# The mixer's output projection as three products of rounded high and low parts, with the normed rows kept whole and divided at the head of the up-projection

## The chip, the cores and the metric

The kernel runs on one core of one Trainium2 chip. The metric is the device time of one launch in microseconds (us). The time before is 4591.77 us, the median of three runs (4585.16 to 4597.04).

## The reference

One inference step of one layer of a hybrid decoder, all in float32: a prompt of 2048 tokens and 8 decode tokens, model width 1024. What matters here is the seam between the token mixer and the feed-forward part:

```python
mixed = jnp.concatenate([o_gdn, o_dsa.astype(o_gdn.dtype)], axis=-1)
x = x + jnp.einsum('bte,ed->btd', mixed, w_out[l])
h = rms_norm(x, norm_ffn[l])
u, ffn_buf = causal_dwconv(jnp.einsum('btd,df->btf', h, w_up[l]), ffn_buf, ffn_conv_w[l])
gate, up = jnp.split(u + ffn_conv_b[l], 2, axis=-1)
x = x + jnp.einsum('btf,fd->btd', jax.nn.silu(gate) * up, w_down[l])
```

`w_out` is 1024 x 1024, `w_up` 1024 x 5632, `w_down` 2816 x 1024.

## The kernel before, in words

The kernel is a row of phases, each a block with its own semaphores and buffers. Between two phases all engines meet in a barrier; SP clears the old phase's semaphores and then, in `credit`, raises each of the new phase's by 4 before its first load. All waits of a phase are for 4 and more.

The phase `mix` (lines 679 to 815) does the output projection, the residual sum, the norm and the transposition. It works on 17 tiles of 128 tokens, sixteen of the prompt and one that holds the 8 decode tokens, with two buffers b = 0, 1 in turn. ScalarE's queue loads `w` (4 MB) whole. For a tile SP loads `m` (the mixed rows, transposed, 512 KB) and `x` (512 KB). TensorE's `multiply` (L730) does for 8 slices k of the contraction and 2 halves of 512 columns one float32 matmul, `m`'s slice stationary and `w` moving. A float32 matmul stands in the trace as two records. VectorE adds the residual (L794), SP stores the sum (L715) and loads the buffer's next `m` and `x`. ScalarE squares and sums (L761), VectorE and ScalarE work out the root and its inverse, VectorE scales the row (L802), TensorE's `turn` (L744) transposes it in 8 pieces, VectorE multiplies by the gain into `h` (L807). ScalarE rounds `h` to the type fp32r into `ht_high` (L767), and POOL writes the rest, `h` less that, to `ht_low` (L781). TensorE's order is multiply(j, 1), turn(j, 0), multiply(j+1, 0), turn(j, 1), in a loop over j; each engine's order is written out by hand in the same way.

The phase `ffn_up` (from L818) makes 22 pairs of 128 gate and up channels. Its weights are loaded 512 KB at a time, rounded by ScalarE (L949 for the first, L926 later) and POOL subtracts (L960). All 2056 token columns are taken in five groups of 412 (the first one 408) in the order 4, 0, 1, 2, 3, each into a PSUM bank of its own, with 8 slices x 3 products of rounded parts (high x high, high x low, low x high, L914). ScalarE empties the banks (L932), and VectorE does the causal convolution. After the third group TensorE transposes some history (`side`, L892), which waits for the first bank to be emptied. `ffn_down` multiplies in the same manner, in the form 128 x 128 weights, 512 moving columns (L1151 to L1153); its weights' low parts come from VectorE (L1161), and those of its activations from POOL (L1123).

## Time and profile before

| | |
|---|---|
| median of three runs | 4591.77 us |
| the profiled execution | 4549.66 us |
| its span, first to last instruction | 4548.4 us |
| mean granted TensorE clock | 0.902 |
| TensorE matmul busy | 3964.1 us, 87% |
| TensorE weight loads busy | 3133.7 us, 69% |
| VectorE busy | 2130.7 us, 47% |
| ScalarE busy | 1527.5 us, 34% |
| GpSimd (POOL) busy | 689.2 us, 15% |

The profile is of one execution. PE is TensorE's matmuls, PEld its weight loads, DVE VectorE, ACT ScalarE, POOL GpSimd, SP the engine that issues most transfers; SPq and ACTq are DMA issues on the queues of SP and ScalarE. "L736" is line 736 of the kernel. After a row's numbers stands in brackets how long the engine was idle ahead of it, and what released it. The granted clock is a share of full speed: 1.00 is 2.4 GHz, 0.50 is 1.2 GHz. The mixer's phase lies between 2713 and 2989 us of the span, the up-projection up to 4000 us, the down-projection behind it.

### The profile page before, as it was taken

What the parts mean: (1) busy time and instruction counts of PE and PEld (TensorE: products, weight loads), DVE (VectorE), ACT (ScalarE), POOL (GpSimd) and SP (SyncE); (2) the same over time, 40 slices, a digit from 0 to 9 for tenths busy, and PEclk for the clock granted to TensorE, in tenths of its full rate; (3) what the DMA queues carried; (4) which work ended last, traced back from release to release, by engine and by line L of the source; (5) the groups of instructions that cost most, each with busy time, mean ns of one, the idle gap of its engine ahead of it and who ended that gap; (6) DMA issues with size and microseconds to landing.
All of it is one profiled execution on the core that took longest, in us unless ns stands there. A gap on an engine that the chain in (4) does not pass through costs nothing. (4 is left out here: it accounts for less than half of the span.)

```text
span 4548.4 us, 51075 instructions
## 1 busy us (share of the span) xinstructions
PE 3964.1 (87%) x19290; PEld 3133.7 (69%) x19290; DVE 2130.7 (47%) x4240; ACT 1527.5 (34%) x2433; POOL 689.2 (15%) x547
## 2 busy tenths in 40 slices
PE   7789787798769876888888769989999999979999
PEld 4445454455358555777777764479999999958777
DVE  5528988998943683333333332224444444430200
ACT  2115555665645233333333321122222222221211
POOL 0100000000000003222222121111111111124443
PEclk9889898999879687778788789999999999989999
DMA  2242222121142102111111013311212121145433
GB/s 92 78 108 64 59 56 69 35 70 36 45 165 73 36 11 69 30 29 33 29 33 31 25 58 107 102 44 37 56 37 56 37 56 37 47 152 168 130 111 112
DMA packets 286836, 298.41 MB, mean 66 GB/s; under 512 B 33599, under 2 KB 231103, under 8 KB 281626
## 3 DMA queue, kind: packets, MB, share of 16 engines
q1 hardware_dynamic: 271278, 256.80, 19.7%
q0 software_dynamic: 2112, 20.97, 1.2%
q10 hardware_dynamic: 13264, 18.25, 1.2%
q8 instruction: 110, 1.80, 0.2%
q14 instruction: 72, 0.59, 0.0%
HBM read 202.15 MB, written 94.10 MB: 65 GB/s over the span
## 5 line engine op out<-in xcount | busy, mean ns | idle before, releaser
L530 PE MATMUL chan_p_g<-ht,chan_w 128*128 128x412 f32 (+1 forms) x1760 | 678.0, 528 | 62.7 <-ACT chan_flat L578 33.7
L914 PE MATMUL up_p_g<-ht_high,up_wh 128*128 128x412 f32 (+1 forms) x1760 | 617.0, 351 | 0.0
L914 PE MATMUL up_p_g<-ht_low,up_wh 128*128 128x412 f32 (+1 forms) x1760 | 615.0, 349 | 0.0
L914 PE MATMUL up_p_g<-ht_high,up_wl 128*128 128x412 f32 (+1 forms) x1760 | 614.8, 349 | 0.0
L530 PEld LDWEIGHTS chan_p_g<-ht,chan_w 128*128 128x128 f32 x1760 | 341.5, 197 | 310.1 <-issue 230.1
L932 ACT ACTIVATE up_pre<-up_p_g 128x412 f32<-128x412 f32 (+1 forms) x220 | 113.3, 515 | 748.0 <-PE up_p_g L914 748.0
L1294 ACT ACTIVATE chan_signed<-chan_sc,chan_trial 128x512 bf16<-128x512 f32 (+6 forms) x224 | 304.9, 1361 | 148.5 <-DVE chan_trial L1349 127.7
L914 PEld LDWEIGHTS up_p_g<-ht_high,up_wh 128*128 128x128 f32 x1760 | 331.3, 188 | 1.6 <-issue 0.4
L914 PEld LDWEIGHTS up_p_g<-ht_low,up_wh 128*128 128x128 f32 x1760 | 331.2, 188 | 1.2
L914 PEld LDWEIGHTS up_p_g<-ht_high,up_wl 128*128 128x128 f32 x1760 | 331.0, 188 | 0.5
L984 DVE TENSOR_SCALAR up_acc<-up_pre,up_taps 128x2048 f32<-128x2048 f32 x44 | 59.3, 1347 | 573.5 <-ACT up_pre L932 573.5
L1335 DVE TENSOR_SCALAR_CACHE_REDUCE chan_tie<-chan_sc,chan_trial 128x384 bf16<-128x384 f32 (+6 forms) x224 | 316.2, 1412 | 7.6
L1270 PE MATMUL chan_p_sc<-ik,chan_iq 128*128 128x512 f32 (+3 forms) x304 | 187.7, 621 | 101.0 <-ACT chan_r L1289 90.9
L1151 PE MATMUL down_p_y<-down_wh,down_ah 128*128 128x512 f32 x704 | 274.4, 390 | 0.0
L1152 PE MATMUL down_p_y<-down_wl,down_ah 128*128 128x512 f32 x704 | 274.2, 390 | 0.0
L1153 PE MATMUL down_p_y<-down_wh,down_al 128*128 128x512 f32 x704 | 274.1, 389 | 0.0
L1123 POOL TENSOR_TENSOR down_al<-down_a,down_ah 128x1024 fp32r<-128x1024 f32 x88 | 211.7, 2405 | 359.8 <-ACT down_ah L1097 359.8
L736 PE MATMUL mix_p_y<-mix_w,mix_m 128*128 128x512 f32 x544 | 237.9, 596 | 22.7 <-DMA mix_m<-scratch_mix 22.7
L960 POOL TENSOR_TENSOR up_wl<-up_w,up_wh 128x1024 fp32r<-128x1024 f32 x44 | 128.7, 2927 | 838.8 <-ACT up_wh L926 830.1
L1289 ACT ACTIVATE chan_r<-chan_p_sc 128x512 f32<-128x512 f32 (+3 forms) x304 | 159.6, 543 | 222.9 <-PE chan_p_sc L1271 115.4
L1097 ACT ACTIVATE down_ah<-down_a 128x1024 fp32r<-128x1024 f32 x88 | 93.3, 1060 | 386.6 <-PE down_p_y L1153 373.6
L736 PEld LDWEIGHTS mix_p_y<-mix_w,mix_m 128*128 128x128 f32 x544 | 102.8, 191 | 146.6 <-issue 146.6
(549 smaller groups left out, 6874.9 us busy)
## 6 DMA issues: line engine op xcount, KB each, us to landing
down_a<-scratch_act SPq DMA_DIRECT2D x88, 512.0 KB, 3.7
scratch_act<-up_acc SPq DMA_DIRECT2D x22, 1028.0 KB, 5.2
up_w<-in_w_up SPq DMA_DIRECT2D x44, 512.0 KB, 6.4
chan_iq<-scratch_iq SPq DMA_DIRECT2D x28, 512.0 KB, 7.2
scratch_qkv<-chan_acc SPq DMA_DIRECT2D x12, 1028.0 KB, 4.6
mid_raw<-scratch_qkv SPq DMA_DIRECT2D x16, 768.0 KB, 5.3
chan_w<-in_w_in SPq DMA_DIRECT2D x22, 512.0 KB, 4.6
proj_x<-in_x_prompt SPq DMA_DIRECT2D x16, 512.0 KB, 3.5
```

The lines of the kernel that those rows point to most:

```text
L530: last = pe.matmul(p_g[u % BANKS][:, 0:cols.stop - cols.start], weights[:, k, :], K.ht[:, k, cols], start=(k == 0), stop=(k == KD - 1))
L736: last = pe.matmul(p_y[b][:, half, :], m[b][:, k, :], w[:, k, half * 512:(half + 1) * 512], start=(k == 0), stop=(k == KD - 1))
L914: last = pe.matmul(p_g[u][:, 0:cols.stop - cols.start], wp[s][:, k, :], hp[:, k, cols], start=(k == 0 and m == 0), stop=(k == KD - 1 and m ...
L960: pool.tensor_tensor(wl[s][:, :, :], w[s][:, :, :], wh[s][:, :, :].bitcast(F32), ALU.subtract).then_inc(s_wl[s], 1)
L1123: pool.tensor_tensor(al[t % RING][:, :, :], a[t % RING][:, :, :], ah[t % RING][:, :, :].bitcast(F32), ALU.subtract)\
L1151: pe.matmul(bank[0:m, :], hi, wh[:, f, :], start=(f == 0), stop=False)
L1152: pe.matmul(bank[0:m, :], hi, wl[:, f, :], start=False, stop=False)
L1153: last = pe.matmul(bank[0:m, :], lo, wh[:, f, :], start=False, stop=(f == NF - 1))
L1270: pe.matmul(out, self.iq[b][:, 0, h, :], self.K.ik2[:, cols], start=True, stop=False)
L1289: act.activation(self.r[n % self.RING][:, 0:width], self.p_sc[n % 2][:, 0:width], ACT.Relu).then_inc(S["relu"], 1)
L1294: act.activation(self.signed[:, 0:nk], self.sc[1][:, 0:nk], ACT.Sign, scale=-1.0, bias=self.trial[:, 1:2].bitcast(F32), accum_out=self.sig ...
L1335: last = dve.tensor_scalar(self.tie[:, 0:na], self.sc[0][:, 0:na], trial[:, 0:1].bitcast(F32), None, ALU.is_ge, ALU.add, accum_out=count[: ...
```

## The change

In `mix` the weights and each tile of `m` are divided into a part rounded to fp32r (ScalarE: `wh`, `mh`) and the rest (VectorE: `wl`, `ml`, written where `w` and `m` had landed). `multiply` does three matmuls of fp32r for each k and half: high x high, high x low, low x high. `w` is loaded in eight slices, and the first tile's multiply waits for them one after the other. There is one buffer `xn` instead of two, and the square's output goes there. POOL has no work left in the phase; `h` and its two parts are gone, and the scaled transposed rows are written whole to `h_full`. In `ffn_up` ScalarE rounds `h_full` in five parts (one per group of columns) into `K.ht`, and VectorE subtracts in place, `K.hl` lying on `h_full`. The first channel pair of TensorE's loop is written out so that each group waits for its own part. `m`'s first loads, the residual loads and the stores stay as they are on SP.

```diff
@@ -681,17 +681,22 @@
 
     with phase(nc, "mix") as (c, stack):
         two = lambda name, shape, dt=F32: [c.sb(f"{name}{b}", shape, dt) for b in range(2)]
-        w = c.sb("w", [P, KD, D])
-        m, x, xn = two("m", [P, KD, P]), two("x", [P, D]), two("xn", [P, D])
-        junk, h = c.sb("junk", [P, D], BF16), c.sb("h", [P, KD, P])
+        with ExitStack() as landing:
+            lands = Ctx(nc, landing, "mix")
+            w = lands.sb("w", [P, KD, D])
+            m = [lands.sb(f"m{b}", [P, KD, P]) for b in range(2)]
+        wl, ml = c.sb("wl", [P, KD, D], F32R), two("ml", [P, KD, P], F32R)
+        wh, mh, x = c.sb("wh", [P, KD, D], F32R), two("mh", [P, KD, P], F32R), two("x", [P, D])
+        xn = c.sb("xn", [P, D])
         stat = two("stat", [P, 4])
         gain = c.sb("gain", [P, KD])
         p_y = [c.ps(f"y{b}", [P, 2, 512]) for b in range(2)]
         p_t = [c.ps(f"t{b}", [P, KD, P]) for b in range(2)]
-        s_w = c.sem("w")
-        s_m, s_x, s_mm, s_x2, s_sum, s_mean, s_root, s_inv, s_norm, s_turn, s_ht, s_st = (
-            c.sems(n) for n in "m x mm x2 sum mean root inv norm turn ht st".split())
-        s_high, s_low = c.sem("high"), c.sem("low")
+        s_w = c.sems("w", KD)
+        s_gain, s_wh, s_wl = c.sem("gain"), c.sem("wh"), c.sem("wl")
+        s_m, s_mh, s_ml, s_x, s_mm, s_x2, s_sum, s_mean, s_root, s_inv, s_norm, s_ht, s_st = (
+            c.sems(n) for n in "m mh ml x mm two sum mean root inv norm ht st".split())
+        s_turn = c.sem("turn")
         block = open_block(nc, stack, c)
         LAST = NT // 2
 
@@ -699,7 +704,7 @@
         def _(sp):
             credit(sp, c)
             sp.dma_start(gain[:, :], norm_ffn.rearrange("(k p) -> p k", p=P), allow_slow_non_contiguous=True)\
-              .then_inc(s_w, 16)
+              .then_inc(s_gain, 16)
 
             def load(j, b, n=P):
                 rows = ds(j * 256 + b * P, P) if n == P else slice(SEQ, TOK)
@@ -728,23 +733,25 @@
 
         @block.tensor
         def _(pe):
-            def multiply(j, b):
-                pe.wait_ge(s_m[b], 4 + j * 16 + 16)
+            def multiply(j, b, first=False):
+                pe.wait_ge(s_ml[b], 4 + j + 1)
                 pe.wait_ge(s_x2[b], 4 + j)
                 for k in range(KD):
-                    for half in range(2):
-                        last = pe.matmul(p_y[b][:, half, :], m[b][:, k, :], w[:, k, half * 512:(half + 1) * 512],
-                                         start=(k == 0), stop=(k == KD - 1))
+                    if first:
+                        pe.wait_ge(s_wl, 4 + k + 1)
+                    for i, (mp, wp) in enumerate(((mh, wh), (mh, wl), (ml, wh))):
+                        for half in range(2):
+                            last = pe.matmul(p_y[b][:, half, :], mp[b][:, k, :], wp[:, k, half * 512:(half + 1) * 512],
+                                             start=(k == 0 and i == 0), stop=(k == KD - 1 and i == 2))
                 last.then_inc(s_mm[b], 1)
 
             def turn(j, b):
                 pe.wait_ge(s_norm[b], 4 + j + 1)
                 pe.wait_ge(s_ht[b], 4 + j)
                 for k in range(KD):
-                    last = pe.transpose(p_t[b][:, k, :], xn[b][:, k * P:(k + 1) * P], K.ident[:, :])
-                last.then_inc(s_turn[b], 1)
-            pe.wait_ge(s_w, 4 + 32)
-            multiply(0, 0)
+                    last = pe.transpose(p_t[b][:, k, :], xn[:, k * P:(k + 1) * P], K.ident[:, :])
+                last.then_inc(s_turn, 1)
+            multiply(0, 0, True)
             with pe.Fori(0, LAST) as j:
                 multiply(j, 1)
                 turn(j, 0)
@@ -754,39 +761,40 @@
 
         @block.scalar
         def _(act):
-            act.dma_start(w[:, :, :], w_out.rearrange("(k p) n -> p k n", p=P)).then_inc(s_w, 16)
+            for k in range(KD):
+                act.dma_start(w[:, k, :], w_out[k * P:(k + 1) * P, :]).then_inc(s_w[k], 16)
+
+            def split(j, b, n=P):
+                act.wait_ge(s_m[b], 4 + j * 16 + 16)
+                act.activation(mh[b][:, :, 0:n], m[b][:, :, 0:n], ACT.Copy).then_inc(s_mh[b], 1)
 
             def stats(j, b):
                 act.wait_ge(s_x2[b], 4 + j + 1)
-                act.activation(junk[:, :], x[b][:, :], ACT.Square, accum_out=stat[b][:, 0:1]).then_inc(s_sum[b], 1)
+                act.wait_ge(s_turn, 4 + j * 2 + b)
+                act.activation(xn[:, :], x[b][:, :], ACT.Square, accum_out=stat[b][:, 0:1]).then_inc(s_sum[b], 1)
                 act.wait_ge(s_mean[b], 4 + j + 1)
                 act.activation(stat[b][:, 2:3], stat[b][:, 1:2], ACT.Sqrt).then_inc(s_root[b], 1)
 
-            def high(j, b, n=P):
-                act.wait_ge(s_ht[b], 4 + j + 1)
-                act.activation(K.ht[:, :, ds(j * 256 + b * P, n)], h[:, :, 0:n], ACT.Copy).then_inc(s_high, 1)
+            split(0, 0)
+            for k in range(KD):
+                act.wait_ge(s_w[k], 4 + 16)
+                act.activation(wh[:, k, :], w[:, k, :], ACT.Copy).then_inc(s_wh, 1)
+            split(0, 1)
             stats(0, 0)
-            with act.Fori(0, LAST) as j:
+            with act.Fori(0, LAST - 1) as j:
+                split(j + 1, 0)
                 stats(j, 1)
-                high(j, 0)
+                split(j + 1, 1)
                 stats(j + 1, 0)
-                high(j, 1)
-            high(LAST, 0, DEC)
-
-        @block.gpsimd
-        def _(pool):
-            def low(j, b, n=P):
-                cols = ds(j * 256 + b * P, n)
-                pool.wait_ge(s_high, 4 + j * 2 + b + 1)
-                pool.tensor_tensor(K.hl[:, :, cols], h[:, :, 0:n], K.ht[:, :, cols].bitcast(F32), ALU.subtract).then_inc(s_low, 1)
-            with pool.Fori(0, LAST) as j:
-                low(j, 0)
-                low(j, 1)
-            low(LAST, 0, DEC)
+            split(LAST, 0, DEC)
+            stats(LAST - 1, 1)
+            stats(LAST, 0)
 
         @block.vector
         def _(dve):
-            dve.wait_ge(s_w, 4 + 32)
+            def lower(j, b, n=P):
+                dve.wait_ge(s_mh[b], 4 + j + 1)
+                dve.tensor_tensor(ml[b][:, :, 0:n], m[b][:, :, 0:n], mh[b][:, :, 0:n].bitcast(F32), ALU.subtract).then_inc(s_ml[b], 1)
 
             def norm(j, b):
                 dve.wait_ge(s_x[b], 4 + j * 16 + 16)
@@ -798,21 +806,32 @@
                 dve.wait_ge(s_root[b], 4 + j + 1)
                 dve.reciprocal(stat[b][:, 3:4], stat[b][:, 2:3]).then_inc(s_inv[b], 1)
                 dve.wait_ge(s_inv[b], 4 + j + 1)
-                dve.wait_ge(s_turn[b], 4 + j)
-                dve.tensor_scalar(xn[b][:, :], x[b][:, :], stat[b][:, 3:4], None, ALU.mult).then_inc(s_norm[b], 1)
-
-            def scale(j, b):
-                dve.wait_ge(s_turn[b], 4 + j + 1)
-                dve.wait_ge(s_low, 4 + j * 2 + b)
-                dve.tensor_tensor(h[:, :, :], p_t[b][:, :, :],
-                                  gain[:, :].unsqueeze(2).broadcast_to([P, KD, P]), ALU.mult).then_inc(s_ht[b], 1)
+                dve.tensor_scalar(xn[:, :], x[b][:, :], stat[b][:, 3:4], None, ALU.mult).then_inc(s_norm[b], 1)
+
+            def scale(j, b, n=P):
+                dve.wait_ge(s_turn, 4 + j * 2 + b + 1)
+                dve.tensor_tensor(K.h_full[:, :, ds(j * 256 + b * P, n)], p_t[b][:, :, 0:n],
+                                  gain[:, :].unsqueeze(2).broadcast_to([P, KD, n]), ALU.mult).then_inc(s_ht[b], 1)
+            lower(0, 0)
+            for k in range(KD):
+                dve.wait_ge(s_wh, 4 + k + 1)
+                dve.tensor_tensor(wl[:, k, :], w[:, k, :], wh[:, k, :].bitcast(F32), ALU.subtract).then_inc(s_wl, 1)
+            lower(0, 1)
+            dve.wait_ge(s_gain, 4 + 16)
             norm(0, 0)
-            with dve.Fori(0, LAST) as j:
+            with dve.Fori(0, LAST - 1) as j:
+                lower(j + 1, 0)
                 norm(j, 1)
                 scale(j, 0)
+                lower(j + 1, 1)
                 norm(j + 1, 0)
                 scale(j, 1)
-            scale(LAST, 0)
+            lower(LAST, 0, DEC)
+            norm(LAST - 1, 1)
+            scale(LAST - 1, 0)
+            norm(LAST, 0)
+            scale(LAST - 1, 1)
+            scale(LAST, 0, DEC)
 
 
 def ffn_up(nc, K, w_up, conv_w, conv_b, conv_state, outs):
@@ -836,7 +855,7 @@
         p_g = [c.ps(f"g{g}", [P, 512]) for g in range(5)]
         p_x = [c.ps(f"x{s}", [P, 2, P]) for s in range(2)]
         p_taps = c.ps("taps", [P, 4, P])
-        S = {n: c.sem(n) for n in ("slab zero tturn taps mm free hist step silu res state").split()}
+        S = {n: c.sem(n) for n in ("parth partl slab zero tturn taps mm free hist step silu res state").split()}
         s_w, s_past, s_st = c.sems("w"), c.sems("past"), c.sem("st")
         s_wh, s_wl, s_conv = c.sems("wh"), c.sems("wl"), c.sems("conv")
         wv = w_up.rearrange("(k p) n -> p k n", p=P)
@@ -900,7 +919,7 @@
                 pe.transpose(p_x[s][0:lead + 2 + DEC, 1, :], pre[s][:, SEQ - lead:SEQ + 2 + DEC], K.ident[:, :])\
                   .then_inc(S["hist"], 1)
 
-            with pe.Fori(0, NF // 2) as j:
+            def channel_pair(j, first=False):
                 for b in range(2):
                     n = j * 2 + b
                     for s in range(2):
@@ -908,6 +927,8 @@
                         parts = ((wh, K.ht), (wh, K.hl), (wl, K.ht))
                         for u, g in enumerate(ORDER):
                             cols = cols_of(g)
+                            if first and b == 0 and s == 0:
+                                pe.wait_ge(S["partl"], 4 + u + 1)
                             pe.wait_ge(S["free"], 8 + n * 10 + s * 5 + u - 4)
                             for k in range(KD):
                                 for m, (wp, hp) in enumerate(parts):
@@ -916,6 +937,9 @@
                             last.then_inc(S["mm"], 1)
                             if u == 2:
                                 side(j, b, s)
+            channel_pair(0, True)
+            with pe.Fori(1, NF // 2) as j:
+                channel_pair(j)
 
         @block.scalar
         def _(act):
@@ -944,9 +968,17 @@
                             act.activation(acc[0][:, :], acc[0][:, :], ACT.Silu).then_inc(S["silu"], 1)
                     if not last:
                         split(n + 1, s)
+            def part(u):
+
+                cols = cols_of(ORDER[u])
+                act.activation(K.ht[:, :, cols], K.h_full[:, :, cols], ACT.Copy).then_inc(S["parth"], 1)
+            part(0)
             for s in range(2):
                 act.wait_ge(s_w[s], 4 + 16)
                 act.activation(wh[s][:, :, :], w[s][:, :, :], ACT.Copy).then_inc(s_wh[s], 1)
+                part(1 + s)
+            part(3)
+            part(4)
             act.wait_ge(S["zero"], 4 + 4)
             with act.Fori(0, NF - 1) as n:
                 copies(n, False)
@@ -961,11 +993,19 @@
 
         @block.vector
         def _(dve):
+            def lower(u):
+
+                cols = cols_of(ORDER[u])
+                dve.wait_ge(S["parth"], 4 + u + 1)
+                dve.tensor_tensor(K.hl[:, :, cols], K.h_full[:, :, cols], K.ht[:, :, cols].bitcast(F32), ALU.subtract)\
+                   .then_inc(S["partl"], 1)
             for s in range(2):
                 dve.memset(pre[s][:, 0:2], 0.0)
             dve.memset(slab[:, :, :], 0.0).then_inc(S["zero"], 2)
             for b in range(2):
                 dve.memset(past[b][:, :, :], 0.0).then_inc(S["zero"], 1)
+            for u in range(5):
+                lower(u)
             dve.wait_ge(S["tturn"], 4 + 1)
             dve.tensor_copy(taps[:, :, :, :].rearrange("p i s m -> p i (s m)"), p_taps[:, :, 0:2 * NF]).then_inc(S["taps"], 1)
             dve.wait_ge(S["taps"], 4 + 1)
@@ -3165,9 +3205,12 @@
                 K.empty = keep("empty", [P, QUARTERS, PAIRS], F32, rule)
                 heads(nc, K, ins, outs)
         with ExitStack() as hidden:
-            K.ht, K.hl = keep("ht_high", [P, KD, TOK], F32R, hidden), keep("ht_low", [P, KD, TOK], F32R, hidden)
+            with ExitStack() as whole:
+                K.h_full = keep("ht_full", [P, KD, TOK], F32, whole)
+            K.hl = keep("ht_low", [P, KD, TOK], F32R, hidden)
             mix(nc, K, ins["x_prompt"].rearrange("b t d -> (b t) d"), ins["x_sample"].rearrange("b t d -> (b t) d"),
                 ins["w_out"].rearrange("l k n -> (l k) n"), ins["norm_ffn"].rearrange("l d -> (l d)"))
+            K.ht = keep("ht_high", [P, KD, TOK], F32R, hidden)
             ffn_up(nc, K, ins["w_up"].rearrange("l k n -> (l k) n"), ins["ffn_conv_w"].rearrange("l j n -> (l j) n"),
                    ins["ffn_conv_b"].rearrange("l n -> (l n)"), ins["state_ffn_conv"].rearrange("l b j n -> (l b j) n"), outs)
         ffn_down(nc, K, ins["w_down"].rearrange("l f n -> (l f) n"), outs)
```

## Rows read from the trace of the kernel before

**Rows 1.** Page, costliest groups: records, busy us, mean ns of one, idle before.
```profile
L1151 PE MATMUL down_p_y<-down_wh,down_ah 128*128 128x512 f32 x704 | 274.4, 390 | 0.0
...
L736 PE MATMUL mix_p_y<-mix_w,mix_m 128*128 128x512 f32 x544 | 237.9, 596 | 22.7 <-DMA mix_m<-scratch_mix 22.7
```

**Rows 2.** Table by stretches: us, each engine's busy us, granted clock, DMA share, GB/s.
```profile
2744.75:2977.46 232.71, 232.71 (x633) 109.49 (x632) 53.73 (x79) 37.48 (x63) 35.24 (x15) 1.00 0.33 100
2977.50:2989.00 11.50, 2.85 (x17) 2.21 (x15) 4.65 (x6) 2.66 (x5) 2.66 (x2) 0.68 0.02 3
3022.00:3044.60 22.60, 22.60 (x124) 22.50 (x123) 8.42 (x7) 6.73 (x8) 2.97 (x1) 1.00 0.00 1
4031.00:4548.00 517.00, 509.83 (x2242) 408.27 (x2241) 68.48 (x55) 110.58 (x107) 209.33 (x87) 1.00 0.44 138
```

**Rows 3.** Timeline, one mixer tile: start us, us, engine, line, operation, count.
```profile
2949.12 13.90 PE L736 MATMUL mix_p_y<-mix_w,mix_m 128*128 128x512 f32 x32
...
2962.86 1.04 PE L744 MATMUL mix_p_t<-ident,mix_xn 128*128 128x128 f32 x8
...
2963.73 13.90 PE L736 MATMUL mix_p_y<-mix_w,mix_m 128*128 128x512 f32 x32
```

**Rows 4.** Timeline, down-projection: products of rounded parts, 48 from first to last.
```profile
4250.01 0.39 PE L1151 MATMUL down_p_y<-down_wh,down_ah 128*128 128x512 f32 x1
4250.02 0.19 PEld L1152 LDWEIGHTS down_p_y<-down_wl,down_ah 128*128 128x128 f32 x1
...
4260.89 0.39 PE L1151 MATMUL down_p_y<-down_wh,down_ah 128*128 128x512 f32 x1
```

**Rows 5.** Timeline, mixer: multiply's end (first transpose), next load of the same buffer.
```profile
2948.25 1.04 PE L744 MATMUL mix_p_t<-ident,mix_xn 128*128 128x128 f32 x8
...
2950.10 0.43 SPq L707 DMA_DIRECT2D mix_m<-scratch_mix  x1
```

**Rows 6.** Answer on the tile mix_m: from issue of a load to landing.
```profile
DMA to landing us min/median/max: 2.9/4.6/8.9
```

**Rows 7.** Groups by shape: whole-tile operations of VectorE and ScalarE.
```profile
L995 DVE TENSOR_TENSOR up_acc<-up_acc 128x2056 f32<-128x2056 f32 x22 | 50.6, 2299 | 0.8
...
L926 ACT ACTIVATE up_wh<-up_w 128x1024 fp32r<-128x1024 f32 x42 | 44.3, 1054 | 0.0
...
L944 ACT ACTIVATE up_acc<-up_acc 128x2056 f32<-128x2056 f32 x22 | 42.4, 1926 | 0.2
```

**Rows 8.** Answer on line 1161: subtraction of 1024 elements, ns min/median/max.
```profile
L1161 DVE TENSOR_TENSOR down_wl<-down_w_next,down_wh x11: 1211/2583/2584, 4234.0 to 4292.0; 128x1024 fp32r<-128x1024 f32 x11
```

**Rows 9.** Timeline, first product of the mixer.
```profile
2729.06 29.43 PE L736 MATMUL mix_p_y<-mix_w,mix_m 128*128 128x512 f32 x64 [22.73 <-DMA mix_m<-scratch_mix]
```

**Rows 10.** Timeline, end of the mixer and head of the up-projection.
```profile
2981.53 1.85 PE L744 MATMUL mix_p_t<-ident,mix_xn 128*128 128x128 f32 x8 [3.03 <-DVE mix_xn L802]
...
2988.01 0.32 POOL L781 TENSOR_TENSOR ht_low<-mix_h,ht_high 128x64 fp32r<-128x64 f32 x1 [1.69 <-ACT ht_high L767]
2989.01 0.09 DVE L965 MEMSET up_pre<- 128x2 f32 x2 [1.37 <-PEq L136]
...
2991.80 1.02 SPq L863 DMA_DIRECT2D up_w<-in_w_up  x2
...
2999.50 0.29 PEld L914 LDWEIGHTS up_p_g<-ht_high,up_wh 128*128 128x128 f32 x1 [0.40 <-issue]
```

**Rows 11.** Timeline, down-projection's first whole products, before the clock rose.
```profile
4031.20 0.63 PE L1151 MATMUL down_p_y<-down_wh,down_ah 128*128 128x512 f32 x1
...
4032.91 0.44 PE L1152 MATMUL down_p_y<-down_wl,down_ah 128*128 128x512 f32 x1
```

**Rows 12.** Timeline of ScalarE, up-projection: table load, first two banks emptied.
```profile
2998.84 1.28 ACT L932 ACT_TABLE_LOAD   x1
3005.50 0.51 ACT L932 ACTIVATE up_pre<-up_p_g 128x408 f32<-128x408 f32 x1 [5.37 <-PE up_p_g L914]
3009.99 0.52 ACT L932 ACTIVATE up_pre<-up_p_g 128x412 f32<-128x412 f32 x1 [3.97 <-PE up_p_g L914]
```

## The prediction

> **What bounds the kernel now.** I began with the page's table of engines and its costliest groups. TensorE is busy for 87% of the span, and the output projection is one of its larger groups: 544 matmul records at L736 with 237.9 us busy, against 704 records each for the down-projection's three products [rows 1]. The mean of one record (596 ns here, 390 ns there) is no price: records overlap, so only the distance from one start to the next is.
>
> Next came the table by stretches [rows 2]. From 2744.75 to 2977.46, the last sixteen of the seventeen tiles, TensorE is busy for 232.71 of 232.71 us at granted clock 1.00, while VectorE has 53.7 us and ScalarE 37.5. The stage is bound by TensorE alone. The up-projection behind it is the same, 22.60 of 22.60 us. Between the two TensorE is nearly idle: 2.85 us busy of the 11.5 from 2977.5 to 2989, and its first product of the up-projection comes only at 2999.50. So four places can move the end: the projection's matmuls, its first tile, its last, and the head of the up-projection.
>
> **Part 1, the steady matmuls.** In the timeline one tile of before runs from 2949.12 to 2963.73, 14.61 us [rows 3]: 32 records in 13.73 us (each single precision matmul leaves two, so 0.429 us apart, 0.858 per product), then eight transposes in 0.87. The new tile issues 16 x 3 = 48 products of rounded parts. The nearest row is the down-projection, same types, 128 weight columns, 512 moving columns: 48 of them go from 4250.01 to 4260.89, 0.2267 us apart [rows 4]. So a tile multiplies in 48 x 0.2267 = 10.88 us instead of 13.73. The bounds of the new pitch: at best that of the old passes halved, 0.429 / 2 = 0.2145 (another 0.6 us per tile); at worst the length of the down-projection's record, 0.389, if loading weights and streaming came one after the other (the first rival). I take 0.2267, because type, shape and engine are the same; that two neighbours here share their weights can only help, and I count nothing for it. Sixteen tiles after the first: 16 x 2.85 = **-45.6 us**, if nothing else becomes late.
>
> What could become late is the operand. From the end of multiply(j, b), in the timeline 2948.25 (the first transpose), to the issue of the next load of the same buffer at 2950.10 are 1.85 us; the landing takes 4.6 us in the median and 8.9 at most [rows 5, 6]. New behind it are ScalarE's rounding (1.05 us, the up-projection's same-sized one) and VectorE's subtraction (1.21 us, shortest record of the down-projection's) [rows 7, 8]. With 0.05 us for each handover the low part is ready 1.85 + 4.6 + 1.1 + 1.3 = 8.8 us after that end. TensorE asks for it after turn, multiply, turn: 0.87 + 10.88 + 0.87 = 12.6 us. There are 3.8 us to spare, and with a landing of 8.9 it would be 0.5 us late. The split stands ahead of the other buffer's statistics in ScalarE's order, and the subtraction ahead of the other buffer's norm in VectorE's; both are done by 8.8 us, and those can't start before that buffer's multiply ends, 0.87 + 10.88 = 11.75 us. The one buffer xn adds a wait of Square for the previous turn, which ends 1.0 us after the multiply, while the residual sum runs: nothing. VectorE's load per tile rises from 3.4 (a sixteenth of 53.7) to some 4.6 of 11.75 us: nothing. The copy and POOL subtraction of the normed rows leave this stage; they held up nobody until its end.
>
> **Part 2, the first tile.** The landing of the first m, which comes after that of w, releases TensorE at 2729.06 [rows 9]. The phase has 38 semaphores instead of 27, each credited by SP ahead of that load. At the up-projection's head 27 clears and 23 credits take at most the 2.8 us from 2989.01 to 2991.80 [rows 10], so 0.056 us each, an estimate: 11 x 0.056 = +0.6. Then three steps that were not there: split of m (1.1), split of w's first slice (1.1), its subtraction behind lower(0,0) (1.3): +3.5. The seven more load issues of ScalarE are done while w is on its way, with ScalarE idle until m has landed: nothing. In exchange the multiply is shorter. Before it took 15.7 us: the last multiply ends at 2963.73 + 13.73 = 2977.46, and sixteen multiplies and fifteen turns earlier is 2744.7; it is 2 us longer than 13.73 because TensorE began at half clock. After, some 3.4 us at half clock give eight products of 0.43 us (the down-projection's first, [rows 11]), the other 40 take 9.1 us: 12.5, so -3.2 (of +4.1). Slices of w come every 1.26 us from VectorE, TensorE uses one in 6 x 0.2267 = 1.36: no wait. Sum **+0.9**.
>
> **Part 3, the last tile.** From the last multiply's end, 2977.46, to the next stage's first memset at 2989.01 are 11.55 us. Its last link is POOL's subtraction of eight columns, done at 2988.33, and 0.68 us go to the barrier [rows 10]. After: the transposes start 4.1 us past the multiply, as now; at half clock they take 1.85, VectorE's scale of eight columns some 0.3 by POOL's 0.32 for as many, barrier 0.7, together 6.95. **-4.6**.
>
> **Part 4, the head of the up-projection.** It counts from that memset. SP clears 11 more semaphores and credits two more: 13 x 0.056 = +0.7 on the w load, whose landing, ScalarE's copy and POOL's subtraction (to 2999.4) set TensorE's start, now 10.5 us in, then 11.2 [rows 10]. part(0) fits in front: ScalarE's 1.054 us for 1024 and 1.926 for 2056 elements [rows 7] give 2.97 us for 3296, so it is through before w lands at 7.6, and VectorE's subtraction (1.21 and 2.30 us [rows 7, 8] give 3.6) by 6.9. The others run beside TensorE, whose groups end 6.0 and then every 4.5 us [rows 12]. Low part 1 is ready at 15.3 against 17.2 needed. Part 2 is rounded by 15.8, but POOL's second subtraction (2.34 us) starts about 15.3, and a VectorE subtraction beside a POOL one has a record of 2.58 us instead of 1.21 [rows 8]; so it is ready between 19.4 and 21.3, against 21.7. Parts 3 and 4 come at 24.9 and 28.5, against 26.3 and 30.8. ScalarE empties the first bank only after part(4), at about 23.6 with the 1.28 us table load [rows 12]; side() asks for that at 26.2. So the pacing costs between 0 and, if three of these overlap with POOL at the doubled length less the spare, 5 us; I take 0, and +0.3 for handovers. **+1.0**. If the cover went (no overlap at all), the four later pieces would be on the path.
>
> **Sum:** -45.6 + 0.9 - 4.6 + 1.0 = -48.3 us. The profiled execution took 4549.66 us (span 4548.4); it becomes about 4501. The median of the runs is 4591.77, 42 us above the profiled one, for which nothing in one trace gives a reason; I take the same difference off it: **4543 us**, -1.05%.
>
> **The rivals.** (A) Weights are not loaded beside the stream. Then 48 x 0.389 = 18.7 us per tile, +4.9 against before; with the first tile and the edges 17 x 4.9 - 3 is about +81, **4673 us**, slower. It decides from a pitch of 13.73 / 48 = 0.286 us. The down-projection's rows speak against it: the load for L1152 starts at 4250.02, 0.01 us after L1151's matmul began, and the next matmul starts 0.22 us later [rows 4]. The Trainium skill, TensorE: Matmul & The Clock Gate, section The mechanism, says that a weight load overlaps a running matmul only when its row group differs, and all loads here use all rows; by that rule the time would be rival A's. By that rule the trace does not agree: 0.2267 us stands against 0.389. Chance 0.03. (B) The operand chain takes over: landings of 8.9 us with the 1.5 MB per tile now moved in 11.75 instead of 14.61 us. 0.5 us late per pair of tiles costs 4; if landings were 12 us, 3.6 per pair, 29: **4572**, still faster. The stage's DMA share of 0.33 speaks against [rows 2]. Chance 0.06. (C) The head of the up-projection runs as if serial, all five parts before the products flow: the four later ones, 4 x 3.6 = 14, and 11 for ScalarE's part behind: up to +25, **4568**. For it: in-order engines, and POOL in between; against it: a wait of its own for each group. Chance 0.05. (D) The clock: 48 products per tile are denser than 32 passes, and if the granted clock of the stage fell to 0.90, 16 x 1.2 = 19 us come back, 4562. The up- and down-projection hold 1.00 with the same products [rows 2]. Chance 0.04. (E) The change gains nothing at all, because the two schedules meet in a wait that no row shows: 4592, chance 0.02.
>
> **How the numbers follow.** My forecast keeps 0.80. The number is its value, 4543. Bounds: pitch 0.2145 gives -10, pacing +5, clock and landings up to +15, and the runs of before spread by 12 us. The range is 4529 to 4560. A measurement can tell about 0.3%, 14 us. Forecast and B to D all gain more than 14: faster 0.94; E: same 0.02; A, with a rest for what I did not see: slower 0.04.
>
> **What would show it.** Starts of the mixer's products 0.227 us apart; tiles every 11.75 us; no idle time of TensorE on the low part of m in the loop; first product about 4 us later than 2729; about 7 us from the last multiply to the next memset; the up-projection's first product 11.2 us after it and no gap between its first five groups. I am wrong if weight loads stand alone between matmuls, if TensorE waits for VectorE's subtraction in the loop, or if the clock row falls under 0.97.

## The result, and the profile after

The changed kernel takes 4541.22 us (median of four runs, 4518.93 to 4545.02), against 4588.55 us for the kernel before in the same comparison. The ratio is 0.9891, 95% interval 0.9865 to 0.9917: 1.1% faster. The prediction was 4543 us, with a range of 4529 to 4560. A second comparison of the two (e7 below) gives 0.9894, 0.9877 to 0.9911.

The two profiled executions differ by 7.6 us of span only (4548.4 and 4540.8). The reason lies ahead of the mixer (e7 below). So the two traces are compared from one mark that both have, ScalarE's first load of the weights (2713.42 before, 2752.38 after), to the first product of the up-projection (2999.50 and 2990.31).

| stretch, us | before | after | change | predicted |
|---|---|---|---|---|
| w load to first residual sum | 31.5 | 33.6 | +2.1 | +0.9 |
| first to last residual sum (16 tiles) | 232.8 | 187.7 | -45.1 | -45.6 |
| last residual sum to next phase's memset | 11.35 | 5.6 | -5.8 | -4.6 |
| memset to the up-projection's first product | 10.5 | 11.05 | +0.6 | +1.0 |
| together | 286.1 | 237.9 | -48.2 | -48.3 |
| first product of the up-projection to the end | 1548.9 | 1550.5 | +1.6 | 0 |

The groups of lines that stand for the single L736 group of before [rows 1], of the kernel after (records, busy us, mean ns of one, idle time ahead):

```profile
L744 PE MATMUL mix_p_y<-mix_wh,mix_mh 128*128 128x512 f32 x272 | 86.4, 399 | 27.3 <-DVE mix_wl L818 27.3
L744 PE MATMUL mix_p_y<-mix_wl,mix_mh 128*128 128x512 f32 x272 | 84.8, 393 | 0.0
L744 PE MATMUL mix_p_y<-mix_wh,mix_ml 128*128 128x512 f32 x272 | 84.7, 393 | 0.0
```

Three groups of 272 stand where 544 records stood; their busy times add up to 256 us, more than the 237.9 of before, though the stage is 45 us shorter. Records of one group overlap those of the next, so the sum counts some stretches more than once, and busy time here says nothing about the gain. The table by stretches of the kernel after (columns as in [rows 2]) has it:

```profile
2752.38:2772.00 19.62, 0.00 (x0) 0.01 (x1) 2.48 (x3) 3.57 (x4) 0.00 (x0) 0.50 0.95 321
2772.00:2785.80 13.80, 13.78 (x49) 11.17 (x50) 8.96 (x8) 6.01 (x7) 0.00 (x0) 0.79 0.00 0
2785.80:2973.50 187.70, 187.70 (x890) 156.53 (x889) 71.03 (x94) 36.75 (x63) 0.00 (x0) 1.00 0.41 123
2973.50:2979.25 5.75, 2.03 (x17) 1.55 (x15) 3.66 (x6) 1.40 (x4) 0.00 (x0) 0.99 0.04 6
...
2990.30:3014.40 24.10, 24.10 (x125) 23.91 (x125) 16.37 (x5) 13.13 (x11) 4.88 (x1) 0.95 0.15 45
```

The third row is the one that answers to the first of [rows 2]: TensorE is busy for all of 187.70 us at clock 1.00, as it was for 232.71, while VectorE rises from 53.7 to 71.0 us and stays far from full. The stage is still bound by TensorE, now with less to do. One tile in the timeline of the kernel after, with the load of its buffer's next m, answers to [rows 3, 5]:

```profile
2938.04 1.03 PE L752 MATMUL mix_p_t<-ident,mix_xn 128*128 128x128 f32 x8
...
2940.18 0.38 SPq L712 DMA_DIRECT2D mix_m<-scratch_mix  x1
...
2944.91 1.06 ACT L769 ACTIVATE mix_mh<-mix_m 128x1024 fp32r<-128x1024 f32 x1 [3.65 <-DMA mix_m<-scratch_mix]
...
2946.00 1.22 DVE L797 TENSOR_TENSOR mix_ml<-mix_m,mix_mh 128x1024 fp32r<-128x1024 f32 x1 [2.62 <-ACT mix_mh L769]
...
2948.45 0.62 PE L744 MATMUL mix_p_y<-mix_wh,mix_mh 128*128 128x512 f32 x2
...
2948.90 0.62 PE L744 MATMUL mix_p_y<-mix_wl,mix_mh 128*128 128x512 f32 x2
...
2949.36 0.62 PE L744 MATMUL mix_p_y<-mix_wh,mix_ml 128*128 128x512 f32 x2
...
2949.82 1.04 PE L752 MATMUL mix_p_t<-ident,mix_xn 128*128 128x128 f32 x8
...
2950.61 0.70 PE L744 MATMUL mix_p_y<-mix_wh,mix_mh 128*128 128x512 f32 x2
```

From transpose to transpose (2938.04 to 2949.82) the tile takes 11.78 us, predicted 11.75. Pairs of products start 0.45 us apart, 0.227 per product. The operand chain reads: multiply's end 2938.04, load issued 2940.18, rounding from 2944.91, subtraction done at 2947.22, needed at 2950.61. That is 9.2 us after the end (predicted 8.8), and 3.4 us early (predicted 3.8).

The edges, in the timeline of the kernel after, head of the mixer first:

```profile
2752.38 3.80 ACTq L765 DMA_DIRECT2D mix_w<-in_w_out  x8
...
2759.70 0.70 SPq L712 DMA_DIRECT2D mix_m<-scratch_mix  x1
...
2768.43 1.06 ACT L769 ACTIVATE mix_mh<-mix_m 128x1024 fp32r<-128x1024 f32 x1 [24.79 <-DMA mix_m<-scratch_mix]
...
2770.66 9.17 DVE L818 TENSOR_TENSOR mix_wl<-mix_w,mix_wh 128x1024 fp32r<-128x1024 f32 x8
```

m's first load is issued 7.3 us after w's (6.7 before), rounded from 2768.43, and w's subtractions start at 2770.66; the first product follows at 2772.0, 19.6 us after the mark where it was 15.6 [rows 9]. Then VectorE's timeline at the mixer's end and the up-projection's head, and TensorE's there:

```profile
2973.67 1.22 DVE L802 TENSOR_TENSOR mix_x<-mix_p_y,mix_x 128x1024 f32<-128x1024 f32 x1 [6.83 <-PE mix_p_y L744]
...
2979.25 0.09 DVE L1003 MEMSET up_pre<- 128x2 f32 x2 [0.36 <-PEq L136]
...
2990.69 3.59 DVE L1000 TENSOR_TENSOR ht_low<-ht_full,ht_high 128x3296 fp32r<-128x3296 f32 x1 [4.98 <-ACT ht_high L974]
2994.49 12.53 DVE L1000 TENSOR_TENSOR ht_low<-ht_full,ht_high 128x3296 fp32r<-128x3296 f32 x3 [0.21 <-ACT ht_high L974]
```

```profile
2989.20 0.71 PEld L908 LDWEIGHTS up_p_taps<-ident,up_slab 128*128 128x128 f32 x4 [10.80 <-DMA up_slab<-in_ffn_conv_b]
...
2990.31 0.71 PE L935 MATMUL up_p_g<-ht_high,up_wh 128*128 128x408 f32 x1
```

The memset comes 5.6 us after the last residual sum and the first product 11.05 us after the memset, behind both the taps' transposes and POOL's subtraction. Low part 0 is ready before that (its subtraction ends at 2985.7), low part 1 at 2994.3 and low part 2 at 3000.0; TensorE comes to group 1 at 2996.0, and the first stretch of the up-projection has TensorE busy for 24.10 of 24.10 us (last row of the table by stretches): the five parts cost nothing.

### The profile page after: what moved, and what is told of

It reads as the page before. It is cut to its first block and busy times, and to the rows that moved or that the text cites. A ratio compares the mean times of both kernels' runs of the same rounds, so it can differ in the third digit from the quotient of the medians.

```text
span 4540.8 us, 51601 instructions
## 1 busy us (share of the span) xinstructions
PE 3943.2 (87%) x19562; PEld 3208.3 (71%) x19562; DVE 2177.8 (48%) x4270; ACT 1550.1 (34%) x2446; POOL 653.1 (14%) x530
## 5 line engine op out<-in xcount | busy, mean ns | idle before, releaser
L530 PE MATMUL chan_p_g<-ht,chan_w 128*128 128x412 f32 (+1 forms) x1760 | 676.3, 528 | 62.9 <-ACT chan_flat L578 33.6
L1208 DVE TENSOR_TENSOR down_x<-down_p_y,down_x 128x512 f32<-128x512 f32 (+1 forms) x34 | 21.0, 680 | 388.0 <-PE down_p_y L1193 388.0
L1361 DVE SCALAR_TENSOR_TENSOR chan_sc<-chan_r,chan_iw,chan_sc 128x512 f32<-128x512 f32 (+3 forms) x266 | 172.6, 683 | 56.3 <-ACT chan_r L1329 54.1
```

Of the source, the lines that this page charges most:

```text
L530: last = pe.matmul(p_g[u % BANKS][:, 0:cols.stop - cols.start], weights[:, k, :], K.ht[:, k, cols], start=(k == 0), stop=(k == KD - 1))
L1361: dve.scalar_tensor_tensor(out=s[:, cols], in0=r, scalar=w, in1=s[:, cols], op0=ALU.mult, op1=ALU.add)\
```

## The experiments

All times of mixers below are from the first to the last residual sum (L802 or its like), sixteen tiles, unless another mark is named.

### e1: float32 products, all else of the change kept

```diff
-for i, (mp, wp) in enumerate(((mh, wh), (mh, wl), (ml, wh))):
-    for half in range(2):
-        last = pe.matmul(p_y[b][:, half, :], mp[b][:, k, :], wp[:, k, ...], ...)
+for half in range(2):
+    last = pe.matmul(p_y[b][:, half, :], m[b][:, k, :], w[:, k, ...], ...)
```
(and without `split`, `lower` and the division of w)

> The changed kernel, but the projection again with one float32 product per slice and half, on w and m as loaded; no rounding and no subtraction in the mixer. All else of the change stays: normed rows kept whole, one xn, the five parts at the head of the up-projection. If the gain is the distance between products (my theory), the mixer's tile is back at 14.6 us instead of 11.78, and the time from the first residual sum to the last at 233 us instead of 188; what is left against the kernel before is the mixer's last tile, about 5 us (0.1%), so the time is some 43 us above the changed kernel and the same as before within what can be told. If the gain came from taking POOL and the copy of the normed rows out of the mixer (rival), tiles stay near 11.8 us and the time stays about 47 us under the kernel before.

Ratio to before 0.9992, 0.9969 to 1.0015: no difference. The answer on the tile mix_p_y of e1 (ns minimum, median, maximum, then first and last start):

```profile
L741 PE MATMUL mix_p_y<-mix_w,mix_m x544: 592/592/1222, 2732.1 to 2979.9; 128*128 128x512 f32 x182
L794 DVE TENSOR_TENSOR mix_x<-mix_p_y,mix_x x17: 1223/1224/1226, 2747.7 to 2980.6; 128x1024 f32<-128x1024 f32 x17
```

The sums run from 2747.7 to 2980.6, 232.9 us, as before. From the w load to the up-projection's first product e1 takes 282.1 us, against 286.1 before and 237.9 for the changed kernel. So 44.2 of the 48.2 us are the products, with the divisions that they need, and 4.0 the new plumbing. The rival, POOL and the copy, falls: with them gone and the float32 products back the tile is 14.6 us again.

### e2: two of the three products

```diff
-for i, (mp, wp) in enumerate(((mh, wh), (mh, wl), (ml, wh))):
+for i, (mp, wp) in enumerate(((mh, wh), (mh, wl))):
```

> The changed kernel with the third product (low part of m times high part of w) left out; everything else, the subtraction that makes that low part too, is as in the changed kernel. TensorE alone would need 32 x 0.2267 + 0.87 = 8.1 us for a tile: 16 x 3.63 = 58 us less than the changed kernel, if it is bound by TensorE. The operand chain (residual sum, store, load of m, rounding, subtraction, and only then the next norm in VectorE's order) takes 9.15 us from one multiply's end to the low part in the changed kernel's trace, and the next residual sum stands behind that subtraction. My theory: the chain takes over, a tile takes 9.2 us, 41 us less than the changed kernel, and TensorE shows about 1 us of idle time per tile, released by VectorE. If the time does not fall by more than 10 us, the products were not what bound the stage.

Measured 140.7 us, 47.0 less than the changed kernel; ratio to before 0.9774, 0.9736 to 0.9812. That is between TensorE's own 58 and the 41 that I had for the chain. Its timeline (one tile, VectorE, SP, ScalarE) and one row of its waits from 2760 to 2880 us (us in total, times, longest):

```profile
2806.61 1.22 DVE L802 TENSOR_TENSOR mix_x<-mix_p_y,mix_x 128x1024 f32<-128x1024 f32 x1
...
2808.54 0.38 SPq L712 DMA_DIRECT2D mix_m<-scratch_mix  x1
...
2813.20 1.06 ACT L769 ACTIVATE mix_mh<-mix_m 128x1024 fp32r<-128x1024 f32 x1 [3.60 <-DMA mix_m<-scratch_mix]
...
2814.30 1.23 DVE L797 TENSOR_TENSOR mix_ml<-mix_m,mix_mh 128x1024 fp32r<-128x1024 f32 x1 [2.58 <-ACT mix_mh L769]
2815.44 1.22 DVE L802 TENSOR_TENSOR mix_x<-mix_p_y,mix_x 128x1024 f32<-128x1024 f32 x1
```

```profile
PE mix_p_y L744 <- DVE mix_ml L797: 6.2, 13, 1.4
```

The residual sum starts the moment the subtraction is over (2806.61, 2815.44: 8.83 us a tile), and TensorE now waits for that subtraction in thirteen cases of this stretch, which it does nowhere in the changed kernel's loop. The chain does take over, at 8.83 and not 9.2 us: when the sum stands behind the subtraction it starts without the 0.27 us that pass after a multiply's end. And it rules only the first 14 of the 16 distances between sums, which add up to 124.7 us, 8.91 each. The last two are 7.88 and 8.17 us: the sum that ends the fifteenth stands behind the division of the eight-token tile (0.22 us), the last sum behind none.

### e3 and e4: a longer operand chain

```diff
+for r in range(2):      # 5 in e4
+    dve.tensor_tensor(pad[b][r][:, :, 0:n], m[b][:, :, 0:n], mh[b][:, :, 0:n].bitcast(F32), ALU.subtract)
 dve.tensor_tensor(ml[b][:, :, 0:n], m[b][:, :, 0:n], mh[b][:, :, 0:n].bitcast(F32), ALU.subtract)
```

> The changed kernel with two more subtractions of the same size (1.22 us each, results unused) ahead of each one that makes m's low part. The chain from a multiply's end to the low part grows from 9.15 to 11.6 us, against 11.75 for VectorE's next residual sum and 12.6 for TensorE. My theory: it fits by 0.15 us, tiles stay at 11.8 us, the mixer gets at most 3 us longer. Rival (the chain already sets the tile): each tile 2.45 us longer, 39 us in all.

> The same with five more subtractions: 9.15 + 6.1 = 15.25 us from a multiply's end to the low part. Each tile's chain then waits for the last one's, as the residual sum stands behind the subtraction in VectorE's order: a tile takes 15.3 us instead of 11.8, the mixer 16 x 3.5 = 56 us more. If the two buffers overlapped their chains (rival: the order of VectorE does not matter), only 15.25 - 12.6 = 2.6 us would be lost for each pair of tiles, 21 us in all.

e3's residual sums, in the answer on its tile mix_p_y:

```profile
L805 DVE TENSOR_TENSOR mix_x<-mix_p_y,mix_x x17: 1215/1225/1225, 2748.6 to 2936.6; 128x1024 f32<-128x1024 f32 x17
```

188.0 us against 187.7: 32 further subtractions on VectorE for 0.3 us. So the changed kernel has room for at least these 2.3 us in this chain. The 2.1 us that e3 gets longer lie in front of the first product (21.6 us after the mark instead of 19.6), where the extra ones stand in the path. e4 takes 226.6 us, 38.9 more; its timeline:

```profile
2862.91 1.21 DVE L805 TENSOR_TENSOR mix_x<-mix_p_y,mix_x 128x1024 f32<-128x1024 f32 x1
...
2869.43 1.06 ACT L770 ACTIVATE mix_mh<-mix_m 128x1024 fp32r<-128x1024 f32 x1 [3.53 <-DMA mix_m<-scratch_mix]
...
2870.53 5.77 DVE L799 TENSOR_TENSOR mix_pad<-mix_m,mix_mh 128x1024 fp32r<-128x1024 f32 x5 [2.50 <-ACT mix_mh L770]
...
2876.21 1.22 DVE L800 TENSOR_TENSOR mix_ml<-mix_m,mix_mh 128x1024 fp32r<-128x1024 f32 x1
2877.35 1.22 DVE L805 TENSOR_TENSOR mix_x<-mix_p_y,mix_x 128x1024 f32<-128x1024 f32 x1
...
2877.56 1.21 PE L745 MATMUL mix_p_y<-mix_wh,mix_mh 128*128 128x512 f32 x2 [2.46 <-DVE mix_ml L800]
```

A tile takes 14.44 us (2862.91 to 2877.35), sum to sum, with the sum right behind the subtraction: the chains don't overlap, as forecast, and the rival's 21 us is off by half. My 56 us were too many for two reasons that e2 shows as well: fourteen tiles and not sixteen, and 14.44 instead of 15.25 us, as five subtractions in a row take 5.77 us, not 6.1, and the sum starts without its delay. 14 x 14.44 + 2 x 12 is 226; in the trace the last two distances are 11.5 and 11.8 us.

### e5: the head of the up-projection in series

```diff
-if first and b == 0 and s == 0:
-    pe.wait_ge(S["partl"], 4 + u + 1)
+if first and b == 0 and s == 0 and u == 0:
+    pe.wait_ge(S["partl"], 4 + 5)
```

> The changed kernel, but TensorE waits at the up-projection's first group for all five parts of the normed rows instead of for its own. In the changed kernel's trace the first product comes 11.05 us after the phase's first memset and the last subtraction ends 27.8 us after it. My theory (the parts run beside TensorE): the first product moves to about 26 to 28 us after the memset, 15 to 17 us later, and the whole is that much longer. Rival: TensorE would have been slowed by the waits group by group anyway, and the whole gets less than 5 us longer.

```profile
2940.57 0.09 DVE L1003 MEMSET up_pre<- 128x2 f32 x2 [0.36 <-PEq L136]
...
2968.49 0.68 PE L935 MATMUL up_p_g<-ht_high,up_wh 128*128 128x408 f32 x1 [16.75 <-issue]
```

In its timeline the first product comes 27.9 us after the memset, 16.9 later than in the changed kernel, and from there to the end it takes 1549.4 us, as long as ever (1550.5). So the five waits are worth 16.9 us; with one wait the change would have brought some 31 us, not 48. This is what rival C was about, at 16.9 instead of 25 us.

### e6: the mixer's first load ahead of the credits

```diff
+sp.dma_start(m[0][:, :, :], K.d_mix[:, :, 0:P].rearrange("k p n -> p k n")).then_inc(s_m[0], 16)
 credit(sp, c)
...
+act.wait_ge(s_turn, 4)
 for k in range(KD):
+    if k == 6:
+        split(0, 0)
     act.wait_ge(s_w[k], 4 + 16)
```
(and the same order on VectorE)

> The changed kernel with another start of the mixer: SP issues the first load of m ahead of its credits, the gain is loaded later, ScalarE and VectorE divide six slices of w ahead of the first tile of m. In the changed kernel the first product comes 19.6 us after ScalarE's first w load is issued; 7.3 us of that is SP on the way to its first m load, 8.7 us the landing. If the landing goes with its own issue: 2.5 us from the load and 1.1 us from the rounding that no longer stands behind m, first product 16.0 us after the w load. If the landing is held up by the traffic of w (4 MB until about 13 us): only 1.1 us, 18.5. Either way 1 to 4 us of 4541, less than a time can tell; the trace is to tell it.

```profile
2713.69 4.42 ACTq L766 DMA_DIRECT2D mix_w<-in_w_out  x8
2718.33 0.38 SPq L705 DMA_DIRECT2D mix_m<-scratch_mix  x1
...
2729.14 1.06 ACT L770 ACTIVATE mix_mh<-mix_m 128x1024 fp32r<-128x1024 f32 x1 [2.36 <-DMA mix_m<-scratch_mix]
...
2731.51 1.22 PE L745 MATMUL mix_p_y<-mix_wh,mix_mh 128*128 128x512 f32 x2 [23.25 <-DVE mix_ml L800]
```

In its timeline the load is issued 2.7 us earlier relative to w's (4.6 instead of 7.3), but the rounding waits until 2729.14, 10.8 us after the issue where it was 8.7. The first product comes 17.8 us after the mark. The landing gave back 2.1 of the 2.7 us: most of the gain is the rounding that no longer queues behind m. Of the two values expected, 16.0 and 18.5, neither is met; 17.8 is nearer to that for a landing held up by other traffic. The time (4505.62 us, ratio 0.990, 0.9846 to 0.9954) can't tell such a difference.

### e7: the changed kernel again

> The changed kernel once more, beside the kernel before on one chip, in five rounds. In the profiled execution of the changed kernel the mixer began 39 us later than in that of before, in code that is the same in both, and all five later profiles put it back at 2714 to 2722 us. If that start is chance, this execution begins the mixer near 2714, its span is near 4501 us (the sum of the prediction), and the ratio to before is near 1 - 48/4555 = 0.9895. If something in the change delays the phases ahead of the mixer, it begins near 2752 again.

4541.17 us against 4585.74, ratio 0.9894. The mixer's mark lies at 2760.1, even later than 2752.4, though e1 to e6 have it at 2714 to 2722. By what was written down this speaks for something in the change; but e5 has the same code as the changed kernel up to the mixer and begins it at 2714.2. So it isn't the change that delays the mixer. The late traces are those of the changed kernel (2752.4), e7 (2760.1), e8 (2742.6) and e9 (2733.8).

Where the time goes, rows with the same work in both show: the stretch from POOL's first indirect load (of 32) to its memset of `state`, and the one from the first to the last update of `state`, each before and after:

```profile
1707.65:1775.46 67.81, 51.09 (x376) 44.59 (x375) 23.95 (x98) 26.57 (x44) 32.66 (x32) 0.88 0.25 71
1893.70:2699.30 805.60, 676.40 (x4394) 611.56 (x4393) 284.39 (x655) 274.97 (x486) 207.92 (x242) 0.82 0.10 28
```

```profile
1711.23:1798.70 87.47, 52.78 (x376) 44.97 (x375) 23.86 (x98) 26.79 (x44) 32.22 (x33) 0.82 0.19 55
1920.30:2737.60 817.30, 689.26 (x4394) 624.52 (x4393) 283.46 (x654) 275.43 (x486) 207.63 (x242) 0.80 0.10 28
```

The same 376 matmuls take 67.8 and 87.5 us, the same 4394 take 805.6 and 817.3 us. In the first stretch TensorE's busy time grows by 1.7 us only (51.1 to 52.8): most of the 19.7 us is not a lower clock but a pause, as TensorE's timeline of the kernel after shows.

```profile
1742.97 1.11 PE L1601 MATMUL step_p_a_t<-ident,step_a_lg 128*128 128x128 f32 x4 [21.98 <-ACT step_a_pt L1672]
```

Its longest pause in that stretch is 22.0 us here, 32.0 in e7 and 29.8 in e8 and e9; in the seven traces that begin the mixer early it is 9.0 or 9.1. So 20 of the 39 us are a pause while POOL issues indirect loads, 12 lie in the second stretch, at a granted clock of 0.80 instead of 0.82, and the rest around them. TensorE waits for ScalarE there, and ScalarE's own idle time of 16.4 us is put down to nothing on this core; what holds it up was not tried. In the comparisons whose trace is late, the kernel before had medians of 4588.6 and 4585.7 us; in the others 4555.1 and 4552.1. That fits executions, or chips, in which this pause is longer; but no late trace of the kernel before exists, so the link is only this agreement.

### e8: both heads reordered

```diff
 for k in range(KD):
+    if k == 2:
+        act.wait_ge(s_turn, 4)
     act.dma_start(w[:, k, :], w_out[k * P:(k + 1) * P, :]).then_inc(s_w[k], 16)
...
+for s in range(2):
+    sp.dma_start(w[s][:, :, :], wv[:, :, s * FF:s * FF + P]).then_inc(s_w[s], 16)
 credit(sp, c)
...
+if first and b == 0 and s == 0 and u == 0:
+    taps_turn()
```
(on top of e6; m's first tile is divided ahead of the third slice of w)

> The early first load (previous run) and with it: ScalarE issues only two slices of w at once and the other six after SP has issued the first load of m; two slices of w are rounded ahead of m, the rest behind; at the up-projection's head SP issues the two weight loads ahead of its credits, and the transposes of the taps move behind the first group. If the traffic of w holds up m's landing, m lands about 4 us after its issue instead of 10.8 and the first product comes 11 to 12 us after the first w load instead of 17.8; if the landing is slow for another reason, it stays above 16. At the up-projection the first product should come 9.5 to 10 us after the memset instead of 11.3. Together 6 to 9 us under the changed kernel, 0.15 to 0.2%, at the edge of what a time can tell.

```profile
2742.56 10.34 ACTq L768 DMA_DIRECT2D mix_w<-in_w_out  x8
2747.20 0.38 SPq L705 DMA_DIRECT2D mix_m<-scratch_mix  x1
...
2754.86 1.04 ACT L772 ACTIVATE mix_mh<-mix_m 128x1024 fp32r<-128x1024 f32 x1
...
2757.59 1.22 PE L745 MATMUL mix_p_y<-mix_wh,mix_mh 128*128 128x512 f32 x2 [22.53 <-DVE mix_ml L801]
```

In its timeline m is being rounded at 2754.86, 7.7 us after its issue and not 10.8. ScalarE was busy with w until then; the answer on the load's own line has the landing itself, 3.9 us after the issue, where e6 has 10.8:

```profile
DMA to landing us min/median/max: 3.9/3.9/3.9
```

So it was the traffic of w that held up m's landing, as expected. The first product comes 15.0 us after the mark instead of 17.8 (e6) and 19.2 (e7). I had expected 11 to 12; ScalarE first issues the held-back slices, so the first two of w are rounded only from 2752.95, m behind them, and TensorE waits for m's low part. The up-projection's first product comes 9.5 us after the memset. Mark to that product: 231.4 us, against 237.3 in e7, so 5.9 us gained on the path. The time is 4531.35 us, ratio 0.9885 (0.9867 to 0.9903): the best three-product version by the trace, but its interval holds that of e7.

### e9: two products without the unused low part

```diff
-dve.wait_ge(s_mh[b], 4 + j + 1)
-dve.tensor_tensor(ml[b][:, :, 0:n], m[b][:, :, 0:n], mh[b][:, :, 0:n].bitcast(F32), ALU.subtract).then_inc(s_ml[b], 1)
...
-pe.wait_ge(s_ml[b], 4 + j + 1)
+pe.wait_ge(s_mh[b], 4 + j + 1)
```
(on top of e2)

> Two products again (the low part of m times the high part of w is left out, so m enters rounded), now without the subtraction that makes the unused low part. With it a tile took 140.7 / 16 = 8.79 us, by the chain through VectorE. Without it the chain is 1.2 us shorter, 7.6 us, and TensorE's 32 x 0.2267 + 0.87 = 8.12 us should set the tile: 130 us from the first sum to the last, 10.8 less. If the chain does not run through that subtraction (rival: the landing of m alone sets it), it stays at 141.

The residual sums, in the answer on its tile mix_x:

```profile
L801 DVE TENSOR_TENSOR mix_x<-mix_p_y,mix_x x17: 1224/1225/1225, 2762.3 to 2892.1; 128x1024 f32<-128x1024 f32 x17
```

2762.3 to 2892.1: 129.8 us, predicted 130. TensorE alone sets the tile again (8.11 us), so the chain of e2 did run through VectorE's subtraction. Ratio 0.9758, 0.9732 to 0.9784. It rounds m, so it buys 58 us with precision.

## Why the prediction was right

**What bounds.** TensorE did bind the mixer, and the price of the change was the distance between starts. Part 1 said 0.2267 us for a product, from the down-projection, and 11.75 us per tile; the trace has 0.227 and 11.78. e1 shows that the gain goes away with the products, and e2 and e9 that the tile follows their number: 11.78 us for three, 8.11 for two. Whoever had multiplied the mean record by the count of a tile (48 x 0.39 = 18.7 us against 32 x 0.596 = 19.1) would have forecast next to nothing, and by the busy time (256 us after, 238 before) a loss.

**Rival A** (weight loads in series, 4673 us) is out: 0.227 us, not 0.389. The Trainium skill, TensorE: Matmul & The Clock Gate, section The mechanism, has a weight load overlap a running matmul only when its row group differs. With that rule taken alone the trace does not agree, in the new loop as little as in the down-projection. The same section also lets a load run ahead when it goes to a background weight buffer; no run here shows whether that is what happens. So the rule as I quoted it was narrower than the section.

**The operand chain** was 0.4 us longer than worked out, 9.2 instead of 8.8. What I got wrong was the point from which it decides. I set its end against TensorE's demand, 12.6 us after the multiply, and called the next statistics safe. The tighter limit is the other buffer's residual sum, which stands behind the subtraction on VectorE: 11.75 us. So the room is about 2.5 us, not 3.8 (11.75 less 9.2; e3 shows that 2.3 fit), and once it is used up each tile pays the whole excess, not each pair (e4: 38.9 us where rival B's arithmetic would give half). With landings of 12 us rival B would have cost more than twice what I wrote, an estimate from these rows: 9.2 + 7.4 - 0.3 = 16.3 us for a tile instead of 11.75, 14 times, is 64 us and not 29. No run here has such landings.

**Part 2** forecast +0.9 and got +2.1 (e7: +1.4). Credits (+0.6) and the three steps (first product 19.6 us after the mark, +4.0 for +4.1) were right. The step that failed is the half-clock time: I carried over 3.4 us from before. In the trace products come 0.43 us apart from 2772.03 to 2777.28, 5.3 us. The first multiply took 13.8 us instead of 12.5, at a mean granted clock of 0.79.

**Part 3** forecast -4.6 and got -5.8. I let the last transposes run at half clock, 1.85 us as in [rows 10]; here they stayed at the full clock (1.09 us, and 1.97 us in e1). e1 shows -4.9 with the old pace, so 0.9 us is the clock and the rest the queue through copy and POOL that is gone.

**Part 4** forecast +1.0, got +0.6. That low part 2 might be late by POOL's doing did not come about: it was ready 20.8 us after the memset, between the 19.4 and 21.3 that I had worked out. But the collision is there: the answer on the subtractions' line (ns minimum, median, maximum) has

```profile
L1000 DVE TENSOR_TENSOR ht_low<-ht_full,ht_high x5: 3559/3578/5524, 2982.2 to 3003.4; 128x3296 fp32r<-128x3296 f32 x4, 128x3264 fp32r<-128x3264 f32 x1
```

one of 5.52 us where the others took 3.6, beside POOL's second subtraction, which took 4.88 us instead of 2.36 (its first). The wait stayed hidden because TensorE takes 4.5 us for a group.

**The median.** Taking the same 42 us off both, I got 4543 for 4541. No row stood behind that step, and that it held is in part luck. They are not launch: a run's time is 1.2 us above its span (4541.99 and 4540.8). The trace of after has 39 us more ahead of the mixer than that of before (e7), which is about their size; that the runs of before lose them in the same place is not shown.

**Luck in the sum.** The parts missed by +0.5, +1.2, -1.2 and -0.4 us, and these cancel to 0.1. The forecast is good to about 1 us a part, not to 0.1. Nine tenths of it rest on part 1, and that one is shown by e1, e2 and e9.

## What to carry to other kernels

Price matmuls by the distance of their starts in a stretch where TensorE never waits, with type and shape alike; record lengths can hide the gain and busy sums can point the wrong way. For an operand that is now divided before use, find the first instruction queued behind the division on its engine: its due time is the limit, not the matmul's. When one profile is set against another, measure between marks that both have; a difference of 39 us in code that nobody touched would have hidden nearly all of a 48 us gain.

## What the runs showed of the hardware

- The same code took 2714 to 2760 us to reach the mixer. While POOL issued 32 indirect loads, TensorE stood still for 9.0 or 9.1 us at a stretch in seven traces and for 22.0 to 32.0 us in four; of the 39 us between the two main traces 20 lie there.
- After a pause the half-clock time differs from execution to execution: the first multiply, the same 48 products behind some 27 and 25 us without work, took 13.8 us in the changed kernel (clock 0.79) and 13.4 in e7 (0.82). In e4 the products behind a pause of 2.46 us inside the loop came 0.43 us apart, at half clock; in the changed kernel the last transposes, behind 3.1 us of waiting, still ran at the full one (1.09 us), and in e5, with the same code up to there and the same wait, at half (1.97 us).
- A load of 512 KB issued 2.7 us earlier beside 4 MB of other traffic landed only 0.6 us earlier (e6); with six of the eight slices held back it landed 3.9 us after its issue instead of 10.8 (e8).
